# One sequence of conv and pool pairs, with two chunks of attention placed inside it

## The reference, cut to what matters

```
x = layer_norm(x, ln0_g, ln0_b)                    # x: 2048 rows of 1024
h = x @ w_in                                       # [value 384 | gate 384 | pool in 384 | queries 256]
a = silu(layer_norm(causal_conv31(h_value * sigmoid(h_gate)) + conv_b))
p = pool_mixer(h_pool)     # trailing means over 2, 4, 8, 16 frames minus the frame, @ pool_w, * pool_scale
m = memory_cross_attention(h_q, mem, w_mk, w_mv)   # 4 heads over 256 memory tokens
x = layer_norm(ALPHA * x + concat(a, p, m) @ w_out, ln1_g, ln1_b)
x = layer_norm(ALPHA * x + conv_ffn(x), ln2_g, ln2_b)
```

## Time and profile before

| | us |
|---|---|
| median of 3 runs (2068.68 to 2076.53) | 2072.58 |
| profiled execution | 2073.64 |
| its span, first to last instruction | 2071.9 |
| PE busy | 1889.2 (91%) |
| DVE busy | 1482.4 (72%) |
| ACT busy | 942.6 (45%) |
| POOL busy | 249.0 (12%) |

### The profile page before, as it was taken

One profiled execution on the slowest core, in us unless ns is written; L12 is line 12 of the kernel. 1 busy time (PEld: TensorE's weight loads), 2 busy tenths in 40 slices (PEclk: granted clock), 3 DMA queues, 4 the chain that ended last, 5 costly groups with the idle time before them and its releaser, 6 DMA issues.

```text
span 2071.9 us, 26056 instructions
## 1 busy us (share of the span) xinstructions
PE 1889.2 (91%) x8626; PEld 1566.7 (76%) x8626; DVE 1482.4 (72%) x1896; ACT 942.6 (45%) x1599; POOL 249.0 (12%) x335
## 2 busy tenths in 40 slices
PE   4999988659999659999999999999999797999997
PEld 4788867548878548888888778888888686887786
DVE  6444028558888468888888788778778767657899
ACT  3111114446556255565556655655566434324231
POOL 1111022111212201222212002000000000000111
PEclk9999999979999879999999999999999999999999
DMA  6432134443353363333343533212223557547543
GB/s 213 152 107 73 45 100 152 132 148 131 123 180 120 117 226 131 140 135 131 142 142 127 198 112 141 93 71 91 81 77 137 193 197 271 188 170 264 183 163 122
DMA packets 171786, 296.12 MB, mean 143 GB/s; under 512 B 11712, under 2 KB 106176, under 8 KB 171712
## 3 DMA queue, kind: packets, MB, share of 16 engines
q1 hardware_dynamic: 171712, 295.18, 40.9%
HBM read 189.23 MB, written 105.91 MB: 142 GB/s over the span
## 4 chain that ended last, share of the span: by engine, by line
PE 55%; DMA 4%; DVE 3%; issue 1%; ACT 1%; SPq 0%; DVEq 0%; ACTq 0%
PE prod_ps L1912 55%; DVE mov_lo L2094 1%; DMA y_scratch<-up_and_out 1%; DMA mov_raw<-wdown_sums_scratch 1%; DMA mov_raw<-x_operands 1%; ACT mov_hi L1959 1%; DVE up_and_out L2128 0%; DVE up_and_out L2125 0%; DMA mov_raw<-in_w_down 0%; DMA mov_raw<-in_ln_b 0%; DVE sta_lo L2090 0%; DMA up_and_out<-x_scratch 0%; ACT sta_hi L1952 0%; ACT prod_ps L1966 0%; DVE sta_raw L2106 0%
## 5 line engine op out<-in xcount | busy, mean ns | idle before, releaser
L1912 PE MATMUL prod_ps<-mov_hi,sta_hi 128*128 128x512 f32 x1848 | 727.0, 393 | 43.4 <-ACT prod_ps L1966 25.3
L1912 PE MATMUL prod_ps<-mov_lo,sta_hi 128*128 128x512 f32 x1848 | 725.1, 392 | 0.0
L1912 PE MATMUL prod_ps<-mov_hi,sta_lo 128*128 128x512 f32 x1848 | 724.5, 392 | 0.0
L1912 PEld LDWEIGHTS prod_ps<-mov_hi,sta_hi 128*128 128x128 f32 x1848 | 350.8, 190 | 121.9 <-ACT prod_ps L1966 27.4
L1912 PEld LDWEIGHTS prod_ps<-mov_lo,sta_hi 128*128 128x128 f32 x1848 | 350.8, 190 | 73.5
L1912 PEld LDWEIGHTS prod_ps<-mov_hi,sta_lo 128*128 128x128 f32 x1848 | 350.6, 190 | 73.3
L2090 DVE TENSOR_TENSOR sta_lo<-sta_raw,sta_hi 128x512 fp32r<-128x512 f32 (+1 forms) x340 | 222.6, 670 | 66.1 <-ACT sta_hi L1952 64.1
L1952 ACT ACTIVATE sta_hi<-sta_raw 128x512 fp32r<-128x512 f32 (+1 forms) x340 | 198.3, 612 | 143.6 <-PE prod_ps L1912 103.0
L259 PE MATMUL wb<-x0t_hi,win_hi 128*128 128x512 f32 x352 | 140.7, 400 | 2.9 <-DVE x0t_lo L351 2.9
L259 PE MATMUL wb<-x0t_hi,win_lo 128*128 128x512 f32 x352 | 138.3, 393 | 0.0
L259 PE MATMUL wb<-x0t_lo,win_hi 128*128 128x512 f32 x352 | 138.1, 392 | 0.0
(11 more groups left out here) (230 smaller groups left out, 2682.2 us busy)
## 6 DMA issues: line engine op xcount, KB each, us to landing
sta_raw<-in_w_up SPq DMA_DIRECT2D x88, 512.0 KB, 4.2
hidden_scratch<-up_and_out SPq DMA_DIRECT2D x44, 512.0 KB, 2.6
y_scratch<-up_and_out SPq DMA_DIRECT2D x16, 1024.0 KB, 7.3
sta_raw<-hidden_scratch SPq DMA_DIRECT2D x32, 512.0 KB, 4.5
up_and_out<-y_scratch SPq DMA_DIRECT2D x16, 1024.0 KB, 4.9
x_operands<-x_operands_out SPq DMA_DIRECT2D x56, 256.0 KB, 4.1
mov_raw<-x_operands SPq DMA_DIRECT2D x14, 1024.0 KB, 6.1
mov_raw<-in_w_down SPq DMA_DIRECT2D x44, 256.0 KB, 4.6
```

The costliest lines, as they stand in the source:

```text
L1912: last = pe.matmul(psum, w, x, start=(start and k == 0 and i == 0), stop=(stop and k == m - 1 and i == 2), skip_group_check=True)
```

## The change

`ORDER` gives the channel pair that stands at each place m of one sequence: conv 0 to 5, then pool 0, conv 6, pool 1, conv 7, ... pool 5, conv 11, then pool 6 to 11. The last conv pair is at place 17 (`last_conv`). Up to there the results rotate over three PSUM banks, after it over two.

The attention of chunk 0 moves from places 13 to 20 to places 8 to 17, and that of chunk 1 from behind the pairs to places 16 to 23. The conv layer norm of chunk 0 moves from places 17 to 22 to behind the pairs. `project(0)` is then written out with the rest of chunk 1's conv layer norm around it. `bands_out` moves from place 8 to 5, `edge_ratios` from 10 to 8, the 4 memsets of keys and values from DVE (place 0) to POOL. The raw taps and their parts exchange buffers; raw w_out rows use the space of the memory inputs (`mc`) first and `r1` only for later rows; `fold` uses other PSUM banks. The diff, cut to its core and moved to the left:

```diff
+HALF_CONV = CONV_PAIRS // 2
+ORDER = (list(range(HALF_CONV)) + [m for i in range(HALF_CONV) for m in (CONV_PAIRS + i, HALF_CONV + i)]
+ + list(range(CONV_PAIRS + HALF_CONV, PAIRS_ALL)))
...
-wo_raw = [r1[:, 0, :], r1[:, 1, :], wo_more[:, 0, :], wo_more[:, 1, :]]
-wo_use = [0, 1, 0, 1, 2, 3, 0, 1]
+flat_mc = [mc[:, i, 0:4, :].rearrange("p k s -> p (k s)") for i in range(2)]
+wo_raw = flat_mc + [wo_more[:, 0, :], wo_more[:, 1, :], r1[:, 0, :], r1[:, 1, :]]
+wo_use = [0, 1, 0, 4, 5, 2, 3, 4]
+wo_sem = [i % 4 for i in wo_use]
...
-taps = r1[:, 0, 0:CONV_GROUPS * TAP_COLS].rearrange("p (n j) -> p n j", j=TAP_COLS)
-tap_parts = prob[:, :, :].rearrange("p u m -> p (u m)")[:, 0:2 * CONV_GROUPS * TAP_COLS].rearrange("p (n e j) -> p n e j", e=2, j=TAP_COLS)
+taps = prob[:, 0, 0:CONV_GROUPS * TAP_COLS].rearrange("p (n j) -> p n j", j=TAP_COLS)
+tap_parts = r1[:, :, :].rearrange("p u m -> p (u m)")[:, 0:2 * CONV_GROUPS * TAP_COLS].rearrange("p (n e j) -> p n e j", e=2, j=TAP_COLS)
...
-fold_bank = [ps_s[:, 0, :], ps_s[:, 1, :], ps_o[:, :]]
+fold_bank = [ps_t[:, 0, :], ps_t[:, 1, :], ps_o[:, :]]
+last_conv = ORDER.index(CONV_PAIRS - 1)
...
+def groups_done(n):
+
+    return 2 * ORDER.index(n // 2) + n % 2 + 1
+
+def bank_of(m):
+    return (ps_y[:, 0, :], ps_y[:, 1, :], ps_m[:, :])[m % 3 if m <= last_conv else m % 2]
...
+        if slot in (2, 3):
             sp.wait_ge(gx_lo, NP)
             sp.wait_ge(edge_x, NP - CONV_PAIRS)
-        if earlier:
...
+        if slot in (4, 5):
+            sp.wait_ge(gt_ok, CONV_GROUPS)
+        if wo_sem[:n].count(wo_sem[n]):
+            sp.wait_ge(wo_l, max(i for i in range(n) if wo_sem[i] == wo_sem[n]) + 1)
...
-        if m >= 4 + CONV_PAIRS:
-            sp.wait_ge(edge_x, m - 3 - CONV_PAIRS)
-        src = cp_d[m * 2 * GROUP:(m + 1) * 2 * GROUP, :].rearrange("(g c) (r q) -> (c r) g q", g=2, r=PHASES)
+            if not is_conv(m - 4):
+                sp.wait_ge(edge_x, pool_no(m - 4) + 1)
...
         else:
-            sp.wait_ge(g_fix, m - CONV_PAIRS + 1)
-        dst = mix_d[m * 2 * GROUP:(m + 1) * 2 * GROUP, :].rearrange("(g c) (r q) -> (c r) g q", g=2, r=PHASES)
+            sp.wait_ge(g_fix, pool_no(m) + 1)
...
-        if m in (4, 5):
-            sp.wait_ge(gt_lo, 2)
-            load_wo(m - 4)
+        if m == 4:
+            sp.wait_ge(prep_lo, 1)
+            load_wo(0)
+            load_chunk(sp, 0, 0, 2 * CT, KT, land[1])
+        if m == 5:
+            sp.dma_start(cln[:, 0, :], a["conv_ln_g"]).then_inc(land[0], 16)
+            sp.dma_start(cln[:, 1, :], a["conv_ln_b"]).then_inc(land[0], 16)
         if m == 6:
-            load_chunk(sp, 0, 0, 2 * CT, KT, land[1])
+            sp.wait_ge(prep_lo, 3)
+            load_wo(1)
+            load_chunk(sp, 1, 1, 2 * CT, KT, early1_in)
         if m == 7:
             load_wo(2)
-        if m == 9:
-            load_wo(3)
         if m:
...
-        if m == 13:
+        if m == last_conv + 1:
             for i, s in enumerate(g_stored):
-                sp.wait_ge(s, 16 * (CONV_PAIRS // 4 + (i == 0)))
+                sp.wait_ge(s, 16 * len(range(i, last_conv + 1, 4)))
+            sp.wait_ge(wo_l, CT)
             load_chunk(sp, 0, 0, 0, CT, land[2])
-        if m == 14:
-            sp.wait_ge(prep_lo, 3)
-            load_chunk(sp, 1, 1, 2 * CT, KT, early1_in)
-            load_chunk(sp, 1, 1, 0, CT, early1_in)
-        if m == 16:
-            sp.dma_start(cln[:, 0, :], a["conv_ln_g"]).then_inc(land[0], 16)
-            sp.dma_start(cln[:, 1, :], a["conv_ln_b"]).then_inc(land[0], 16)
+            load_chunk(sp, 1, 1, 0, CT, land[1])
+        if m == last_conv + 2:
+            load_wo(3)
+            load_wo(4)
     store_pair(NP - 1)
...
-    for n in range(4, 6):
-        load_wo(n)
+    load_wo(5)
+    load_wo(6)
...
-    load_wo(6)
     load_wo(7)
...
+    for x in (kt_hi, kt_lo, v_hi, v_lo):
+        link(pool.memset(x[:, :, :, :].bitcast(mybir.dt.uint32), 0))
...
+    for j in range(NP - CONV_PAIRS):
+        m, i = ORDER.index(CONV_PAIRS + j), j * 2 * GROUP // POOL_GROUP
+        x, y = lead_x[:, j, :, :], g_res[:, m % 4, :, 0:2]
...
-        if m >= CONV_PAIRS:
+        if m > last_conv:
             pe.wait_ge(g_out, 2 * m - 2)
         elif m >= 3:
             pe.wait_ge(g_out, 2 * m - 4)
...
+        if m == 8:
+            pe.wait_ge(kv_lo, 2 * QT)
+            scores(0, 0)
         if m == 9:
             fold(0)
+        if m == 10:
+            scores(0, 1)
         if m == 11:
             fold(1)
         if m == 13:
             pe.wait_ge(fold_lo, 2 * CT)
-            scores(0, 0)
+            turn(0, 0)
         if m == 15:
-            scores(0, 1)
+            turn(0, 1)
         if m == 16:
-            turn(0, 0)
+            scores(1, 0)
         if m == 17:
+            attend(0)
+        if m == 18:
+            scores(1, 1)
+        if m == 19:
+            turn(1, 0)
+        if m == 21:
+            turn(1, 1)
+        if m == 23:
             mean(0)
-        if m == 18:
-            turn(0, 1)
-        if m == 20:
-            attend(0)
+            pe.wait_ge(o_lo, 1)
+            attend(1)
             variance(0)
 
     pe.wait_ge(g_out, NG)
...
-    pe.wait_ge(o_lo, 1)
...
-    chunk(1, 1, 0)
+    mean(1)
+    pe.wait_ge(wo_l, KT)
+    project(0, 0, 0)
+    project(0, 0, 1)
+    variance(1)
+    project(0, 0, 2)
+    project(0, 0, 3)
+    turn_x1(0, 0)
...
-            act.wait_ge(gt_ok, CONV_GROUPS)
+            act.wait_ge(gt_lo, 2)
...
-        act.wait_ge(bands, 3 + 2 * sum(POOL_LAGS) + len(POOL_LAGS))
+        act.wait_ge(bands, 7 + 2 * sum(POOL_LAGS) + len(POOL_LAGS))
...
-            act.wait_ge(prep_zero, 8)
+            act.wait_ge(bands, 7)
...
             act.activation(wv_hi, r_wv, ACT.Copy).then_inc(prep_hi, 1)
+            bands_out()
         if m == 6:
...
         if m == 7:
             values_out()
+            query_hi(0, 0)
+        if m == 8:
             wout_hi(1)
-        if m == 8:
             wout_hi(2)
-            bands_out()
         if m == 9:
-            query_hi(0, 0)
+            exps(0, 0)
         if m == 10:
             fold_out(0)
+        if m == 11:
+            exps(0, 1)
         if m == 12:
             fold_out(1)
...
         if m == 14:
-            exps(0, 0)
+            turned_hi(0, 0)
         if m == 16:
-            exps(0, 1)
+            turned_hi(0, 1)
         if m == 17:
-            turned_hi(0, 0)
+            exps(1, 0)
+        if m == 18:
+            attn_hi(0, 0)
         if m == 19:
-            turned_hi(0, 1)
-            squares(0, 0)
-        if m == 21:
-            attn_hi(0, 0)
-            deviation(0)
+            exps(1, 1)
+        if m == 20:
+            turned_hi(1, 0)
         if m == 22:
-            act.wait_ge(land[0], 48)
-            swish(0, 0)
+            turned_hi(1, 1)
+    squares(0, 0)
     wout_hi(3)
-    query_hi(1, 1)
     wout_hi(4)
+    attn_hi(1, 1)
+    deviation(0)
     wout_hi(5)
+    act.wait_ge(land[0], 48)
+    swish(0, 0)
+    wout_hi(6)
     pooled_hi(0, 0)
-    wout_hi(6)
     wout_hi(7)
...
+    squares(1, 1)
+    query_hi(2, 0)
+    deviation(1)
+    norm(0, 0)
+    swish(1, 1)
+    pooled_hi(1, 1)
+    turned_x1(0, 0)
...
+            dve.wait_ge(g_mm, groups_done(n - 3))
...
-        conv_band(2 * m + 3)
-        conv_band(2 * m + 4)
+        if is_conv(m):
+            conv_band(2 * ORDER[m] + 3)
+            conv_band(2 * ORDER[m] + 4)
         if m + 3 < NP:
             pair_lo(m + 3)
-        if m == 0:
-            for x in (kt_hi, kt_lo, v_hi, v_lo):
-                dve.memset(x[:, :, :, :].bitcast(mybir.dt.uint32), 0).then_inc(prep_zero, 1)
...
+            query_low(0, 0)
+        if m == 8:
             wout_lo(1)
-        if m == 8:
             wout_lo(2)
+            edge_ratios()
         if m == 9:
-            query_low(0, 0)
+            maxima(0, 0)
         if m == 10:
+            normalise(0, 0)
             fold_low(0)
-            edge_ratios()
...
         if m == 12:
+            normalise(0, 1)
             fold_low(1)
+        if m == 13:
+            query_low(1, 1)
...
-            normalise(0, 0)
+            turned_lo(0, 0)
         if m == 16:
-            maxima(0, 1)
+            turned_lo(0, 1)
         if m == 17:
-            normalise(0, 1)
-            turned_lo(0, 0)
-            conv_total(0, 0)
+            maxima(1, 0)
         if m == 18:
-            deviations(0, 0)
+            normalise(1, 0)
+            attn_lo(0, 0)
         if m == 19:
-            turned_lo(0, 1)
-            square_sum(0)
-        if m == 21:
-            attn_lo(0, 0)
-            scale_conv(0, 0)
+            maxima(1, 1)
+        if m == 20:
+            normalise(1, 1)
+            turned_lo(1, 0)
         if m == 22:
-            conv_lo(0, 0)
+            turned_lo(1, 1)
+    conv_total(0, 0)
+    deviations(0, 0)
+    square_sum(0)
     wout_lo(3)
-    query_lo(1, 1)
     wout_lo(4)
+    attn_lo(1, 1)
+    scale_conv(0, 0)
     wout_lo(5)
```

(29 more changed lines are left out.)

58 lines of the change are left out of this document (28 added, 30 removed).

## The result

The changed kernel takes 2063.84 us (median; 2062.09 to 2065.26), the kernel before 2075.18 in the same session: ratio 0.995, 95% interval 0.9935 to 0.9964, so 7 to 13 us faster. The forecast was 2060.0. Of the miss of 3.8, 2.6 is that the kernel before read higher in that session than the 2072.58 shown; against its own neighbour the gain is 11.3, forecast 12.6.

What follows compares the result with a forecast made beforehand. No engine's load but engine-to-engine chains and PE's slow clock after idling bound the first 179.8 us. Gains 2.4 + 3.9 + 6.1 = 12.4 take the profiled 2073.6 to 2061.2, the median to 2060; range 2052 to 2072.

Steps and rivals of the forecast that it cites:

- The sum: First conv product to chunk 2's scores: gains at last pair 2.4, tail 3.9 and project(0) 6.1, together 12.4 us.
- the ledger: Same stretch as 116.0 work, 41.3 idle, 8.1 slow clock and 1.9 small hops between engines: 167.3 us, before 179.8.
- Project(0), 6.1: From project(0) to chunk 2's scores: 25.7 us instead of 31.8, including one slow start of 2.8; gain 6.1.
- Tail, 3.9: From the last pair to project(0): 18.7 us instead of 22.6, w_out's rows not last; gain 3.9.
- Last pair at 425.4: End of the last pair, walked through the queues: about 425.4 instead of 427.8, a gain of 2.4 us.
- SP's late start: store_pair(6) and load_pair(12) wait on SP for edge_ratios' chain; pair 12 lands 5 us after it, scores(0,1) waits 2.9.
- the slow clock: PE running under 2.4 GHz after idling: 8.1 us forecast, before 14.7, including values 2.3, after turn(1,1) 1.4, project(0) 2.8.
- Memsets, cost none: Four memsets on POOL, 0.9 to 2.3 us each, covered by 9 us at least and not delaying DVE's band products.
- Longer chains: Rival: about 25 hops on PE's path each 0.3 us longer, gain only 5, 2068 us; chance 0.28.
- The clock: Rival: frequent waits hold PE at 1.2 GHz from values through attend(0), 25 us slower, 2098; chance 0.07.
- Better: Rival: no low clock at values and turn(1,1), SP's delay hidden; 6.6 us more gain, 2053; chance 0.13.
- Bound by loads: Rival: w_out row 7 lands 3 us later, losing 3 of the tail's 3.9: 2063 us, inside the forecast's range.

Runs made afterwards that it cites:

- The second run with idle products: Changed kernel plus 26 matrix products with unused results on PE behind variance(0) and 18 behind mean(1): 2058.91 us, ratio 0.9924 to the kernel before.
- the early split: Changed kernel with the split of w_mv and the rounding of the pool bands moved from place 5 to 3: 2057.72 us, ratio 0.9922 to the kernel before.
- the last kernel: Changed kernel with w_mv's split, bands and edge_ratios in place 3, norm parameters' wait in place 20, chunk 1's attention behind the pairs: 2042.96 us, ratio 0.985.

## Why the prediction came out as it did

**The sum.** Its three terms were 2.4 + 3.9 + 6.1 = 12.4; the profile has 0.7 + 3.0 + 6.0 = 9.7. The forecast of 2060 is near the 2063.84, but in the ledger behind it two errors stand against each other: slow clock and hops took 17.9 where 10.0 was forecast, and idle time 36.6 where it was 41.3. Part of that is mechanism, as told below; that it left only 3.2 is luck.

*Project(0), 6.1.* Right: 25.86 from its start to the scores of chunk 2, forecast 25.7, slow start included. The second run with idle products gives that start 2.7; the sum had 2.8.

*Tail, 3.9.* It took 19.6 instead of 18.7. The walk left out that a table load waits with its instruction when two waits stand in front. The 0.9 missing is accounted for: taking one wait away gave 1.0. That the rows of w_out are not last held: DVE's split of the last one ends the wait.

*Last pair at 425.4.* It ended at 427.1. The waits themselves, in order (forecast, then trace): 2.4 and 2.27; 2.4 and 1.54; 3.7 and 3.70; 2.5 and 1.43; 2.9 and 3.05; 2.9 and 1.01; 2.3 and 1.88; 1.7 and 1.80; 0.7 and 0.49; 5.0 and 5.23; 2.4 and 1.97; 12.4 and 7.34 + 4.83. Sum 41.3 and 36.5. So the walk through the queues holds; its one wait off by over 1.1 is at scores(0,1), SP's late start, where the trace has two courses, 1.0 and 4.7, on either side of 2.9.

**The step that failed is the slow clock**, and its price is the ledger's: 8.1 of slow clock and 1.9 of hops forecast, 17.9 measured. The places it named were right (values 8.3 for 6.0, as forecast; turn(1,1); project(0)). It missed pair 6 (2.04 for 1.0), which then covered 1.0 of the next wait, scores(0,0) (2.9 for 1.6) behind a wait of 3.05 that it had judged by the 2.96 of the earlier trace rows, keys (7.3 for 6.0) and the conv products ahead of them behind 2.27, and turn(0,0). Part of the slow clock filled waits, which is why idle came out 4.7 below the forecast while the sum was 3.2 above.

The prediction also had a better price at hand. In the kernel before, 14.7 of slow clock go with 49.1 of idle time, a share of 0.30; on the 41.3 forecast that is 12, not 8.1. Of the 14.7 the prediction placed 4.5 (half of 5.29 and of 3.7), and it passed over the wait of 4.45, behind which the clock fell a microsecond late. In the changed kernel the share is 0.49, and with the early split (14.1 of 31.1) and in the last kernel (10.6 of 23.6) 0.45.

One row at full clock behind 2.96 was made a rule; the kernel with the memsets alone had the same 2.96 with half clock. The Trainium skill (TensorE: Matmul & The Clock Gate, on psum-queue depth-cycling) says that frequent micro-idles can make the clock oscillate. The prediction held against this at 2.96. The later runs side with the Trainium skill: with more and shorter waits the slow clock rose from 14.7 to 17.9. None shows by what measure.

**Memsets, cost none.** Right. Each took 0.95 (bounds 0.9 and 2.3), the bands were ready at 329.7 (326 to 331), and DVE's band beside them took 1.49, while beside POOL's selects it takes 1.60:

```profile
301.31 0.95 POOL L816 MEMSET values_hi<- 128x1024 uint32 x1
301.90 1.49 DVE L1454 TENSOR_TENSOR wout_hi<-x_out,ln_gb 128x1280 fp32r<-128x1280 f32 x1
312.39 1.60 DVE L1454 TENSOR_TENSOR wout_hi<-x_out,ln_gb 128x1280 fp32r<-128x1280 f32 x1
```

A memset reads nothing, a select does. What the Trainium skill's section on contending engines, cited ahead for this, states agrees with both. The selects now run until 329.7 and stretch DVE's operations for longer, but that cost nothing here: keys started 0.3 ahead of the forecast, and DVE then stood idle for 5.38, waiting for PE:

```profile
332.40 1.49 DVE L1454 TENSOR_TENSOR wout_lo<-x_out,ln_gb 128x1280 fp32r<-128x1280 f32 x1 [5.38 <-PE y_ps L958]
```

That values start 1.0 late is again the slow clock: keys took 7.3 instead of 6.0, and pair 5 ended at 337.6 instead of 336.7.

**The stations.** Keys 323.2 (323.5), values 344.8 (344), scores of chunk 2 at 472.5 (470), the longest wait among pairs at turn(1,1): held. Scores(0,1) at about 3 didn't, nor 18 to 19 for the tail (19.6). The granted clock between 352 and 404 was 0.93, not under the 0.9 that was named as a sign of being wrong; it fell at two places only, 0.50 at scores(0,0) and again at turn(0,0). DVE, not a load, ended the wait in front of project(0).

**The rivals.** "Longer chains" was wrong in mechanism: hops didn't add. "The clock" came true in kind, not in its place or price: slow stretches of 2 to 5 us behind single waits, 3.2 in all over the kernel before, and full clock again in between. "Better" would have needed the opposite. "Bound by loads" did not occur.

**What the sum couldn't tell** is which part pays. Not every part does. Each taken by itself in the changed kernel, in the profile and by the ratios: the memsets gain 3.5 (5), the mixed pairs cost 3.3 (4), chunk 1 among pool pairs costs 6.6 (6), and w_mv's split, left at place 5, costs 9.3 (6). The second and the last are two ways to the same slack and don't add.
